# Routing by pairs of heads, a share of the expert rows on VectorE, and a respaced schedule in a two-layer diffusion step

## The chip, the cores and the metric

The kernel runs on one core of a Trainium2 chip. The metric is the device time of one execution in microseconds (us). Three runs of the kernel before took 2585.73, 2594.09 and 2606.0 us; the median, 2594.09 us, is the time that the change is held against.

## What is computed

The reference is one step of a two-layer network on 128 context tokens and 256 latent tokens, all in float32 with a model width of 1024. Each layer modulates its input, mixes the tokens (three parallel groups of heads: neighbourhood attention, grouped-query attention, a Fourier mix), projects, adds and normalizes; then it does the same with a mixture of small experts (PEER) in place of the token mix:

```python
x <- LN(ALPHA*x + gate1 * TokenMix(x*(1+scale1)+shift1))
x <- LN(ALPHA*x + gate2 * PEER(x*(1+scale2)+shift2))

q = (xt @ w_q).reshape(n, PEER_HEADS, 2, PEER_QHALF)          # 8 heads, 2 halves
s = jnp.einsum('nhpc,hpkc->nhpk', q, sub_keys)                # 128 keys per half
top_s, top_i = lax.top_k(s, 16)
cand_s = top_s[:, :, 0, :, None] + top_s[:, :, 1, None, :]    # 256 pairs per head
cand_i = top_i[:, :, 0, :, None] * 128 + top_i[:, :, 1, None, :]
best_s, best_j = lax.top_k(cand_s.reshape(n, 8, -1), 16)
experts = jnp.take_along_axis(cand_i.reshape(n, 8, -1), best_j, axis=-1)
gates = jax.nn.softmax(best_s, axis=-1)
a = einsum('tkd,td->tk', u_tab[experts], x)                   # 128 experts per token
y = einsum('tk,tkd->td', gates * gelu(a), v_tab[experts])
```

Each token so picks 128 of 16384 experts, and each expert is one row U (dotted with the token) and one row V (summed with the resulting weight). The six shift, scale and gate vectors of a layer come from a product of a conditioning vector with a 1024 x 6144 matrix ("modulation").

## The kernel before

**Blocks and stages.** The tokens stand in six blocks of 128: blocks 0 (context), 1 and 2 (latent) in layer 0, and blocks 3, 4 and 5, the same tokens in layer 1. A token mix runs once per layer for the context block and once for the two latent blocks together, so there are four mixes; the latent ones work on two blocks at once. A block's expert part has 128 "slots": slot k gathers, for each of its 128 tokens (one per partition), the k-th expert's U and V row, 8 KB, into one of the eight places of a ring (`uv_rows`, RING = 8, lines 358 and 585 to 592). The gathers are indirect transfers that GpSimd issues in order, and each waits until the place that it fills is free (line 588).

**What happens to a slot.** VectorE dots the U half with the token (`expert_dots`, line 1206); ScalarE makes the GELU, the weight and a diagonal matrix of the weights (`expert_weights`, lines 885 to 894); TensorE multiplies that diagonal with the V half and sums in PSUM in `acc` (`experts_sum`, lines 698 to 704), which also frees the slot. Two slots are one turn; TensorE is two turns behind (BEHIND). A block has 64 turns, numbered 0 to 63, and two more in which only TensorE works. The block's last step is `ln2` (line 1068): it waits for the sum and normalizes.

**The order of the work.** One list, SCHEDULE, is written out when the kernel is built (lines 152 to 204), and every engine goes through this same list in order, doing its own part of each step and waiting on semaphores. So each engine's instructions follow the order of the list, and a wait holds up all that stands behind it on that engine. The steps are `mod` (a tile of the modulation), `xT` (transpose and modulate), `proj` (an input projection tile), `norm`, `qkT`, `att`, `four`, `oT`, `gate`, `outp` (an output tile), `ln1`, `h2`, `wq` (a query tile of one head, and the key scores of the head before it), `top` (the 16 best of four lists of scores), `pick` (the routing's later part), `ln2` and `gather` (some turns of a block). `beside(q, steps, behind)` lays the turns of block q between the given steps: a fixed cost per kind of step (COST) says how far the turns must have come at each step, and `behind` turns are left over at the end. `filled_in` puts `mod` steps behind given kinds of steps (FILL). Beside block 0 stands the mix of blocks 1 and 2 and their queries; beside block 1 the routing of block 2, what is left of the modulation and the start of the mix of block 3; beside block 2 the rest of that mix and the queries; beside block 3 the mix of blocks 4 and 5; beside block 4 the routing of block 5; beside block 5 nothing.

**Routing.** For each pair of heads, `top` searches four lists and `pick` 0 to 3 adds the scores of 2 x 16 x 16 pairs and searches the best 16 per head (lines 1147 to 1154). Only then, for all eight heads at once, `pick` 4 and 5 turn the found positions into expert numbers by comparing with 0 to 15, multiplying and summing (lines 1159 to 1170), and make the gates. One signal, `route_ready`, then releases all 128 slots of the block to GpSimd (lines 581 and 1180).

**Weights.** SyncE issues the weight tiles of 1 MB in the order of the list into three places (`wtiles`). Up to the first gather the eight places of the ring serve as further weight places: the first EARLY_TILES tiles may use them, and GpSimd waits until these tiles are used (lines 311 and 583).

Of the kernel before, what the change touches and what calls it, by code (L numbers as in the profile page):

```python
# [31 lines left out]
U32 = mybir.dt.uint32  # L32
# [5 lines left out]
P = 128  # L38
# [12 lines left out]
PER_TOKEN = R_H * TOPK  # L51
ALPHA = (2 * DEPTH) ** 0.25
# [71 lines left out]
def query_steps(m):  # L124
# [7 lines left out]
    return steps + [("pick", q, 4), ("pick", q, 5)]  # L132


def route_steps(q):

    return [s for n in range(4) for s in (("top", q, n), ("pick", q, n))] + [("pick", q, 4), ("pick", q, 5)]
# [9 lines left out]
def cost(step):  # L147
    by_mix = step[0] in ("proj", "att", "outp", "wq", "four")
    return COST[step[0]][by_mix and len(BLOCKS[step[1]]) - 1] + 3 * (step[0] == "pick" and step[2] >= 4)

# [123 lines left out]
ROUTE = numbered(("pick",), lambda s: [s[1]] if s[2] == 5 else [])  # L274
# [10 lines left out]
def routes_before(step):  # L285

    return sum(s[0] == "pick" and s[2] == 5 for s in SCHEDULE[:SCHEDULE.index(step)])
# [23 lines left out]
EARLY_TILES = sum(s in TILES for s in SCHEDULE[:SCHEDULE.index(("xT", BLOCKS[1][0]))])  # L311
# [35 lines left out]
def hybrid_step(nc, i, o):  # L347

    ctx = ExitStack()
    with ctx:  # L350
# [42 lines left out]
        half_j = sb("half_j", [P, PER_TOKEN], U32)  # L393
        half_f = sb("half_f", [P, PER_TOKEN])
        picked = sb("picked", [P, 2, PER_TOKEN])
# [617 lines left out]
        def _(dve):  # L1013
# [127 lines left out]
            def pick_experts(q, part):  # L1141
# [29 lines left out]
                if part < 5:  # L1171
                    return
# [183 lines left out]
```

## Time and profile before

| | us |
|---|---|
| median of three runs | 2594.09 |
| profiled execution | 2596.99 |
| span of its one core | 2595.2 |
| TensorE busy (share of the span) | 2175.1 (84%) |
| VectorE busy | 1471.3 (57%) |
| ScalarE busy | 839.9 (32%) |
| GpSimd busy | 855.1 (33%) |
| bytes moved | 962.04 MB, mean 371 GB/s |

The profile is of one execution, and its page gives busy times per engine and the span in 40 slices of 64.9 us. Other views show single instructions in order of time, sums over stretches of time, groups of like instructions, and who waited for whom. PE is TensorE's matmuls, DVE is VectorE, ACT is ScalarE, POOL is GpSimd, SP is SyncE. A wait is shown in brackets behind the instruction that it delayed. PEclk is the granted TensorE clock as a share of 2.4 GHz.

### The profile page before, as it was taken

The numbers are of one execution on the slowest core, as the hardware profiler recorded it, in microseconds if no ns is written. First come the engines' busy times: TensorE is split into PE (matmuls) and PEld (weight loads), VectorE is DVE, ScalarE is ACT, GpSimd is POOL, SyncE is SP. The second block draws the span as 40 slices with busy tenths as digits, with TensorE's granted clock in tenths as the row PEclk, the third lists the DMA queues.
The fourth block names the chain that finished last, engine by engine and source line by source line (L and its number), as shares of the span: only waits on it lengthen the run. The fifth ranks groups of instructions, "written<-read, shape, count | busy, mean of one in ns | idle before, by whom it ended". The sixth has DMA issues, their size and how long they took to land.

```text
span 2595.2 us, 22854 instructions
## 1 busy us (share of the span) xinstructions
PE 2175.1 (84%) x7370; PEld 1179.5 (45%) x7370; DVE 1471.3 (57%) x3171; ACT 839.9 (32%) x2632; POOL 855.1 (33%) x772
## 2 busy tenths in 40 slices
PE   7997999899687888798887799999968786777775
PEld 5585655566232344354443465567523332323222
DVE  0146456456788544545668446644786767544444
ACT  2423366232222232443222237622222222222222
POOL 0001235222244443233444124422324444343331
PEclk8797999999798999899998899999979898999998
DMA  9958989799799999999999699979979999999996
GB/s 397 369 202 357 334 341 412 294 388 373 285 387 421 395 421 421 374 373 418 419 420 392 255 348 369 415 283 362 361 272 416 422 420 395 378 423 421 421 422 252
DMA packets 142631, 962.04 MB, mean 371 GB/s; under 512 B 15920, under 2 KB 24240, under 8 KB 28208
## 3 DMA queue, kind: packets, MB, share of 16 engines
q0 software_dynamic: 110592, 805.36, 76.7%
q1 hardware_dynamic: 30912, 152.06, 15.3%
q10 hardware_dynamic: 1008, 3.17, 0.3%
q8 instruction: 58, 0.95, 0.1%
q14 instruction: 61, 0.50, 0.0%
HBM read 958.17 MB, written 2.36 MB: 370 GB/s over the span
## 4 chain that ended last, share of the span: by engine, by line
PE 49%; DMA 26%; DVE 15%; issue 5%; ACT 3%; POOL 0%; SPq 0%; DVEq 0%; POOLq 0%; ACTq 0%
PE acc L701 27%; DMA uv_rows<-in_peer_uv,experts 25%; PE pair L757 8%; PE pair L816 6%; DVE products L1206 3%; PE pair L721 2%; PE pair L794 1%; PE pair L642 1%; DVE arena L1132 1%; PE pair L620 1%; DMA uv_rows<-in_w_mod 1%; ACT weight L889 1%; PE pair L731 1%; DVE arena L1167 1%; DVE arena L1169 1%
## 5 line engine op out<-in xcount | busy, mean ns | idle before, releaser
L701 PE MATMUL acc<-uv_rows,diag 128*128 128x512 f32 x3072 | 1474.6, 632 | 274.5 <-ACT diag L893 274.3
L589 POOL DMA_INDIRECT uv_rows<-in_peer_uv,experts x768 | 854.9, 1113 | 1702.2 <-PE acc L701 1372.2
L1206 DVE CUSTOM_DVE_ANT_0 products<-uv_rows,h_tok 128x1024 bf16<-128x1024 f32 x768 | 940.9, 1225 | 741.4 <-DMA uv_rows<-in_peer_uv,experts 730.5
L701 PEld LDWEIGHTS acc<-uv_rows,diag 128*128 128x128 f32 x3072 | 602.1, 202 | 1088.0 <-issue 677.0
L885 ACT ACTIVATE gelu<-dots 128x2 f32<-128x2 f32 x384 | 78.3, 204 | 1220.7 <-DVE dots L1206 1220.3
L893 ACT ACTIVATE diag<-consts,weight 128x128 f32<-128x128 f32 x768 | 260.2, 386 | 0.0
L757 PE MATMUL pair<-wtiles,hT 128*128 128x256 f32 x976 | 220.7, 385 | 13.3 <-ACT hT L849 13.3
L757 PEld LDWEIGHTS pair<-wtiles,hT 128*128 128x128 f32 x976 | 188.7, 194 | 52.9 <-issue 28.0
L889 ACT ACTIVATE weight<-gelu,gates 128x1 f32<-128x1 f32 x768 | 184.3, 287 | 12.6
L835 ACT COPY arena<-pair 128x256 f32<-128x256 f32 (+3 forms) x154 | 83.4, 549 | 281.0 <-PE pair L757 109.6
L816 PE MATMUL pair<-hT,wtiles 128*128 128x256 f32 (+1 forms) x864 | 154.2, 337 | 0.0
L816 PEld LDWEIGHTS pair<-hT,wtiles 128*128 128x128 f32 x864 | 137.9, 191 | 22.9 <-issue 10.5
L794 PE MATMUL pair<-arena,consts 128*128 128x512 f32 x40 | 34.1, 1004 | 51.5 <-DVE arena L1190 51.5
L885 ACT ACT_TABLE_LOAD x51 | 65.4, 1283 | 0.9
L1206 DVE DVE_READ_ACCUMULATOR2_ANT dots<- 128x1 f32 x768 | 63.1, 82 | 0.0
L721 PE MATMUL pair<-uv_rows,cond_s 128*32 128x256 f32 x576 | 53.8, 513 | 4.5 <-DMA uv_rows<-in_w_mod 2.1
L1031 DVE TENSOR_REDUCE maxes<-pair 128x2 f32<-128x768 f32 (+1 forms) x36 | 28.1, 780 | 50.6 <-PE pair L620 50.2
L864 ACT ACT_TABLE_LOAD x31 | 39.8, 1283 | 36.1 <-DVE neg_max L1032 36.0
L731 PEld LDWEIGHTS pair<-consts,mod_row 128*128 128x128 f32 x192 | 34.1, 256 | 35.8 <-issue 15.2
L1126 DVE MAX8 top_s<-arena 128x8 f32<-128x128 f32 x96 | 20.9, 280 | 49.1 <-ACT arena L835 49.0
L731 PE MATMUL pair<-consts,mod_row 128*128 128x2 f32 x192 | 37.1, 303 | 13.0 <-ACT mod_row L835 12.9
L1088 DVE TENSOR_REDUCE root_in<-arena 128x10 f32<-128x640 f32 x6 | 4.9, 820 | 72.7 <-ACT arena L946 72.7
(113 smaller groups left out, 1192.5 us busy)
## 6 DMA issues: line engine op xcount, KB each, us to landing
uv_rows<-in_w_mod SPq DMA_DIRECT2D x36, 1024.0 KB, 14.2
wtiles<-in_peer_wq SPq DMA_DIRECT2D x27, 1024.0 KB, 5.7
wtiles<-in_w_in SPq DMA_DIRECT2D x24, 1024.0 KB, 9.6
wtiles<-in_w_out SPq DMA_DIRECT2D x15, 1024.0 KB, 6.9
wtiles<-in_w_mod SPq DMA_DIRECT2D x12, 1024.0 KB, 12.3
uv_rows<-in_peer_uv,experts POOLq DMA_INDIRECT x768, 11.0
rows<-in_ln_g SPq DMA_DIRECT2D x12, 512.0 KB, 7.9
rows<-in_ln_b SPq DMA_DIRECT2D x12, 512.0 KB, 11.1
```

Source lines behind the costliest of these rows:

```text
L589: pool.indirect_dma_start(out=uv_rows[:, slot, :, :].rearrange("p t d -> p (t d)"), out_offset=None, in_=i["peer_uv"], in_offset=bass.Indi ...
L701: last = nc.tensor.matmul(acc[:, half, :], diag[:, slot, :], uv_rows[:, slot, 1, half * 512:(half + 1) * 512], start=False, stop=True, ski ...
L721: last = nc.tensor.matmul(dst[at:at + QUADRANT, 0, 0:TW], cond_s[:, k, :], w[:, k, :], start=(k < GROUPS_OF_PE), stop=(k >= NC - GROUPS_OF ...
L731: last = nc.tensor.matmul(dst[:, 0, 2 * k:2 * k + 2], mod_row[:, (t - 1) % 2, k * P:(k + 1) * P], const("halves"), start=True, stop=True)
L757: last = nc.tensor.matmul(dst, hT[:, k, b * P:(b + 1) * P], w[:, k, :], start=(k == 0), stop=(k == NC - 1))
L794: last = nc.tensor.matmul(dst[:, n, :], ones, z[:, n * 512:(n + 1) * 512], start=True, stop=True)
L816: last = nc.tensor.matmul(dst[:, h, 0:t], w[:, k, h * P:(h + 1) * P], hT[:, k, 0:t], start=(k == 0), stop=(k == NC - 1))
L835: last = nc.scalar.copy(out, src)
L885: nc.scalar.activation(gelu[:, slot:slot + G], dots[:, slot:slot + G], ACT.Gelu).then_inc(gelu_ready, 1)
L889: nc.scalar.activation(weight[:, slot + j:slot + j + 1], gelu[:, slot + j:slot + j + 1], ACT.Copy, scale=gates[:, q % 3, at:at + 1]).then_ ...
L893: nc.scalar.activation(diag[:, slot + j, :], ident, ACT.Copy, scale=weight[:, slot + j:slot + j + 1]).then_inc(diag_ready, 1)
L1206: nc.vector.tensor_tensor_reduce(out=products[:, :], in0=uv_rows[:, slot, 0, :], in1=h_tok[:, slot_q, :], scale=1.0, scalar=0.0, op0=ALU.m ...
```

## The change

Four things change.

1. A pair of heads is routed to its end in one `pick` step: position, expert numbers and gates of its 32 slots, from an area of 1024 elements instead of 2048 done twice. Each of the four steps signals `route_ready`, and GpSimd waits for it at every 32nd slot. The steps `pick` 4 and 5 are gone.
2. In blocks 0 and 3, of every four slots the last (n % 4 == 3) has its V row summed by VectorE in SBUF (`dve_sum`), one turn later, in place of the diagonal on ScalarE and the four matmuls on TensorE. `ln2` of these blocks adds the two sums.
3. The gathers of block 0 begin behind its first `pick`, with the other query and routing steps of that block laid between its turns. The weight places in the ring are given up before the first `wq` (EARLY_TILES is 43 instead of 64), so that the `wq` tiles have three places.
4. COST is changed, `behind` is 6, 1, 6, 6 and 6 instead of 2, 0, 3, 2 and 3, and no `mod` steps stand behind `top` and `pick` any more. Of the 48 modulation tiles 13 leave the start and 3 leave block 1; these 16 stand in block 2 now, between `oT` and `gate`, turns 10 to 25.

Unrolled, the list has so many turns of the block ahead of these steps (before / after). Block 0: first projection 0 / 10, attention from 9 to 33 / 19 to 33, output tiles 36 to 39 / 35 to 38, queries of blocks 1 and 2 from 44 / 43, last `pick` 62 / 58. Block 3: attention 12 to 35 / 14 to 30, output tiles 37 to 40 / 32 to 35, queries from 45 / 41, last `pick` 62 / 58. Beside block 0 after, each `top` and its `pick` for blocks 1 and 2 stand together, with two turns, a `wq`, a turn, a `wq` and a turn up to the next `top`; beside blocks 2 and 3 after, one turn or none stands between a `top` and its `pick`; beside blocks 1 and 4, three and five.

```diff
+PARTS = 4
+PER_PART = PER_TOKEN // PARTS
+PART_H = R_H // PARTS
...
-COST = {"mod": (3, 3), "bias": (2, 2), "xT": (3, 3), "proj": (4, 6), "norm": (4, 6), "qkT": (2, 2), "att": (3, 12),
-        "four": (0, 0), "kvout": (0, 0), "oT": (1, 1), "gate": (3, 3), "gate2": (0, 0), "outp": (4, 7),
-        "ln1": (3, 3), "h2": (4, 4), "wq": (4, 8), "top": (4, 4), "pick": (5, 5), "ln2": (4, 4)}
+COST = {"mod": (3, 3), "bias": (2, 2), "xT": (3, 3), "proj": (4, 7), "norm": (6, 6), "qkT": (3, 3), "att": (3, 8),
+        "four": (1, 2), "kvout": (0, 0), "oT": (2, 2), "gate": (3, 3), "gate2": (0, 0), "outp": (4, 7),
+        "ln1": (4, 4), "h2": (3, 3), "wq": (5, 8), "top": (5, 5), "pick": (9, 9), "ln2": (4, 4)}
...
-FILL = {"kvout": 1, "qkT": 1, "att": 2, "four": 1, "ln1": 3, "h2": 1, "top": 2, "pick": 5}
+FILL = {"kvout": 1, "qkT": 1, "att": 2, "four": 1, "ln1": 3, "h2": 1}
...
-    last = queries.index(("wq", 0, R_H))
-    s += filled_in(mix_end(0), fill, FILL) + queries[:last + 1] + filled_in(queries[last + 1:], fill, FILL)
-    s += beside(0, mix_start(1) + mix_middle(1) + mix_end(1) + query_steps(1), 2)
-
-    s += beside(1, route_steps(2) + fill + mix_start(2))
-    s += beside(2, mix_middle(2) + mix_end(2) + query_steps(2), 3)
-    s += beside(3, mix_start(3) + mix_middle(3) + mix_end(3) + query_steps(3), 2)
-    s += beside(4, route_steps(5), 3)
+    first = queries.index(("pick", 0, 0)) + 1
+    s += filled_in(mix_end(0), fill, FILL) + queries[:first]
+    s += beside(0, queries[first:] + mix_start(1) + mix_middle(1) + mix_end(1) + query_steps(1), 6)
+
+    before_mix, after = [t for t in fill if t[2] < PART_G1 or t[1] == 0], [t for t in fill if t[1] and t[2] >= PART_G1]
+    s += beside(1, route_steps(2) + before_mix + mix_start(2), 1)
+    s += beside(2, mix_middle(2) + after + mix_end(2) + query_steps(2), 6)
+    s += beside(3, mix_start(3) + mix_middle(3) + mix_end(3) + query_steps(3), 6)
+    s += beside(4, route_steps(5), 6)
...
+SHARED_WITH_DVE = (0, 3)
+def summed_by_dve(n):
+    return n // PER_TOKEN in SHARED_WITH_DVE and n % 4 == 3
...
-EARLY_TILES = sum(s in TILES for s in SCHEDULE[:SCHEDULE.index(("xT", BLOCKS[1][0]))])
+EARLY_TILES = sum(s in TILES for s in SCHEDULE[:SCHEDULE.index(("wq", 0, 0))])
...
-                pool.wait_ge(route_ready, ROUTE[q])
...
+                    if k % PER_PART == 0:
+                        pool.wait_ge(route_ready, PICK[(q, k // PER_PART)])
                     if n >= RING:
-                        pool.wait_ge(row_used, n - RING + 1)
+                        by_pe, by_dve = summed_before(n - RING + 1)
+                        if summed_by_dve(n - RING):
+                            pool.wait_ge(row_added, by_dve)
+                        else:
+                            pool.wait_ge(row_used, by_pe)
...
-                elif kind == "pick" and a[1] == 4:
-                    act.wait_ge(best_ready, ROUTE[a[0]])
+                elif kind == "pick":
+                    act.wait_ge(best_ready, PICK[a])
                     nc.scalar.activation(gate_e[:, :, :], gate_e[:, :, :], ACT.Exp).then_inc(gate_exp, 1)
...
+                        if q in SHARED_WITH_DVE:
+                            dve.wait_ge(row_added, summed_before(PER_TOKEN * (q + 1))[1])
+                            nc.vector.tensor_tensor(zz, acc[:, :, :], dve_sum[:, :].rearrange("p (a n) -> p a n", a=2),
+                                                    ALU.add).then_inc(acc_drained, 1)
+                            dve.wait_ge(acc_drained, q + 1)
+                            link(nc.vector.tensor_tensor(zz, zz, gate_b, ALU.mult))
...
+                top_sixteen([(flat[:, h], best_s[:, PART_H * part + h], best_j[:, PART_H * part + h]) for h in range(PART_H)])
+                nc.vector.tensor_tensor(gate_e[:, :, :], best_s[:, heads, :], spread(best_s[:, heads, 0:1], [P, PART_H, TOPK]),
+                                        ALU.subtract).then_inc(best_ready, 1)
+                nc.vector.tensor_copy(top_f[:, :, :], top_i[:, lists, :])
+                nc.vector.tensor_scalar(half_j[:, :, 0, :], best_j[:, heads, :], 4, None, ALU.logical_shift_right)
+                link(nc.vector.tensor_scalar(half_j[:, :, 1, :], best_j[:, heads, :], 15, None, ALU.bitwise_and))
+                link(nc.vector.tensor_copy(half_f[:, :], half_j[:, :, :, :].rearrange("p h f k -> p (h f k)")))
+                by_slot = hit.rearrange("p (n a) -> p n a", a=TOPK)
+                link(nc.vector.tensor_tensor(by_slot, spread(half_f[:, :].unsqueeze(2), [P, 2 * PER_PART, TOPK]),
+                                             spread(iota.unsqueeze(1), [P, 2 * PER_PART, TOPK]), ALU.is_equal))
...
+                dve.wait_ge(gate_exp, PICK[(q, part)])
...
+                def add_rows(h):
+                    for n in range(q * PER_TOKEN + h * G, q * PER_TOKEN + (h + 1) * G):
+                        if not summed_by_dve(n):
+                            continue
+                        slot, before = n % RING, summed_before(n)[1]
+                        dve.wait_ge(weight_ready, n + 1)
+                        if before:
+                            dve.wait_ge(row_added, before)
...
+                            nc.vector.scalar_tensor_tensor(out=dve_sum[:, :], in0=uv_rows[:, slot, 1, :],
+                                                           scalar=weight[:, slot:slot + 1], in1=dve_sum[:, :],
+                                                           op0=ALU.mult, op1=ALU.add).then_inc(row_added, 1)
...
+                    if 1 <= h <= GROUPS:
+                        add_rows(h - 1)
```

## Rows read from the trace of the kernel before

**Rows 1.** Page, GB/s per slice of 64.9 us, and all transfers

```profile
GB/s 397 369 202 357 334 341 412 294 388 373 285 387 421 395 421 421 374 373 418 419 420 392 255 348 369 415 283 362 361 272 416 422 420 395 378 423 421 421 422 252
...
DMA packets 142631, 962.04 MB, mean 371 GB/s; under 512 B 15920, under 2 KB 24240, under 8 KB 28208
```

**Rows 2.** Stretches, blocks 0 to 4: length, busy per engine, clock, DMA, GB/s

```profile
234.00:709.00 475.00, 434.71 (x1573) 270.95 (x1571) 267.56 (x575) 188.72 (x502) 152.97 (x136) 0.95 0.89 348
...
709.00:1061.00 352.00, 284.81 (x704) 129.48 (x704) 225.58 (x489) 97.74 (x357) 146.08 (x129) 0.92 1.00 409
...
1061.00:1446.00 385.00, 321.07 (x987) 165.25 (x987) 235.98 (x515) 125.41 (x406) 148.79 (x128) 0.91 0.98 395
...
1446.00:1921.00 475.00, 433.22 (x1579) 270.39 (x1578) 272.47 (x580) 187.34 (x498) 143.65 (x128) 0.95 0.86 331
...
1921.00:2255.00 334.00, 257.20 (x520) 104.61 (x520) 222.06 (x480) 87.67 (x327) 145.02 (x128) 0.91 0.99 407
```

**Rows 3.** Waits of GpSimd: us in total, times, longest

```profile
POOL uv_rows L589 <- DVE gates L1179: 52.0, 2, 26.4
```

**Rows 4.** Timeline, GpSimd, first gather: start, us, engine, line

```profile
233.64 1.07 POOL L589 DMA_INDIRECT uv_rows<-in_peer_uv,experts  x1 [233.19 <-PE pair L721]
```

**Rows 5.** Timeline, VectorE: routing of block 0, first dot product

```profile
177.85 0.69 DVE L1151 TENSOR_TENSOR arena<-top_s 128x512 f32<-128x512 f32 x1
...
182.92 0.88 DVE L1126 MAX8 top_s<-arena 128x8 f32<-128x128 f32 x4
...
188.26 0.69 DVE L1151 TENSOR_TENSOR arena<-top_s 128x512 f32<-128x512 f32 x1
...
230.83 0.29 DVE L1179 TENSOR_TENSOR gates<-gate_e,gate_n 128x128 f32<-128x128 f32 x1
...
239.76 1.22 DVE L1206 CUSTOM_DVE_ANT_0 products<-uv_rows,h_tok 128x1024 bf16<-128x1024 f32 x1 [8.65 <-DMA uv_rows<-in_peer_uv,experts]
```

**Rows 6.** Timeline, TensorE: a turn, a query tile, two attention steps

```profile
488.12 3.60 PE L701 MATMUL acc<-uv_rows,diag 128*128 128x512 f32 x8
...
562.27 7.07 PE L816 MATMUL pair<-hT,wtiles 128*128 128x256 f32 x32
...
569.17 1.05 PE L825 MATMUL pair<-sktiles,arena 128*128 128x128 f32 x8
...
1094.13 0.49 PE L620 MATMUL pair<-kT,qT 64*128 64x128 f32 x4 [2.07 <-ACT arena L835]
...
1100.50 0.49 PE L620 MATMUL pair<-kT,qT 64*128 64x128 f32 x4
```

**Rows 7.** Groups by line and form: busy us, mean ns of one

```profile
L1071 DVE SCALAR_TENSOR_TENSOR arena<-x_tok,arena 128x1024 f32<-128x1024 f32 x12 | 14.7, 1225 | 0.4
...
L849 ACT ACTIVATE hT<-pair,mod_cols 128x128 f32<-128x128 f32 x96 | 34.5, 472 | 15.8 <-PE pair L610 15.8
```

**Rows 8.** Stretches of block 0, and the attention of block 3

```profile
240.00:315.00 75.00, 73.65 (x277) 53.92 (x278) 35.17 (x63) 22.26 (x57) 17.52 (x15) 0.96 0.97 362
...
315.00:458.00 143.00, 139.64 (x537) 77.17 (x538) 82.42 (x152) 90.76 (x223) 66.10 (x53) 0.99 0.93 371
...
537.00:648.00 111.00, 111.00 (x437) 77.52 (x436) 67.78 (x208) 28.26 (x92) 28.91 (x29) 1.00 0.97 377
...
648.00:709.00 61.00, 38.74 (x68) 15.46 (x66) 42.66 (x94) 14.45 (x41) 16.17 (x17) 0.78 0.70 279
...
1541.00:1682.00 141.00, 139.37 (x551) 77.39 (x549) 82.44 (x152) 93.76 (x230) 64.24 (x54) 1.00 0.97 382
```

**Rows 9.** Timeline, VectorE, block 4: last routing step to next dot

```profile
2185.35 0.22 DVE L1165 TENSOR_SCALAR half_j<-best_j 128x128 uint32<-128x128 uint32 x1
...
2194.31 1.22 DVE L1206 CUSTOM_DVE_ANT_0 products<-uv_rows,h_tok 128x1024 bf16<-128x1024 f32 x1
```

**Rows 10.** Stretch behind that step

```profile
2200.00:2210.00 10.00, 10.00 (x23) 4.35 (x23) 5.54 (x10) 3.22 (x13) 4.69 (x5) 0.94 0.84 302
```

**Rows 11.** Timeline, TensorE behind a wait, end of block 3

```profile
1885.83 6.01 PE L701 MATMUL acc<-uv_rows,diag 128*128 128x512 f32 x8 [8.96 <-ACT diag L893]
```

More of the change, by code:

```diff
@@ L148, in cost @@
     by_mix = step[0] in ("proj", "att", "outp", "wq", "four")
-    return COST[step[0]][by_mix and len(BLOCKS[step[1]]) - 1] + 3 * (step[0] == "pick" and step[2] >= 4)
+    return COST[step[0]][by_mix and len(BLOCKS[step[1]]) - 1]
 def beside(q, steps, behind=0):
@@ L285, in routes_before, with summed_before @@
 def routes_before(step):
-    return sum(s[0] == "pick" and s[2] == 5 for s in SCHEDULE[:SCHEDULE.index(step)])
+    return sum(s[0] == "pick" for s in SCHEDULE[:SCHEDULE.index(step)])
+SHARED_WITH_DVE = (0, 3)
+def summed_by_dve(n):
+    return n // PER_TOKEN in SHARED_WITH_DVE and n % 4 == 3
+def summed_before(n):
+    by_dve = sum(summed_by_dve(k) for k in range(n))
+    return n - by_dve, by_dve
 def mix_of(q):
@@ L1142, in pick_experts @@
                 l, slot = q // 3, q % 3
-                c4 = cand.rearrange("p (h a b) -> p h a b", h=R_H, a=TOPK)
-                top4 = top_s[:, :, :].rearrange("p (h f) k -> p h f k", f=2)
-                shape = [P, R_H, TOPK, TOPK]
-                top_f = scores[:, place_in_mix(q), 0:2 * R_H * TOPK].rearrange("p (h f k) -> p h f k", f=2, k=TOPK)
-                if part < 4:
-                    heads = slice(2 * part, 2 * part + 2)
-                    two = [P, 2, TOPK, TOPK]
-                    link(nc.vector.tensor_tensor(c4[:, heads], spread(top4[:, heads, 0, :].unsqueeze(3), two),
-                                                 spread(top4[:, heads, 1, :].unsqueeze(2), two), ALU.add))
-                    flat = cand.rearrange("p (h n) -> p h n", h=R_H)
-                    top_sixteen([(flat[:, h], best_s[:, h], best_j[:, h]) for h in (2 * part, 2 * part + 1)])
@@ L1171, in pick_experts @@
-                if part < 5:
-                    return
-                link(nc.vector.scalar_tensor_tensor(out=picked[:, 0, :], in0=picked[:, 0, :], scalar=float(KEYS),
-                                                    in1=picked[:, 1, :], op0=ALU.mult, op1=ALU.add))
-                link(nc.vector.tensor_scalar(experts[:, slot, :], picked[:, 0, :], float(l * EXPERTS), None, ALU.add))
-                dve.wait_ge(gate_exp, ROUTE[q])
+                heads = slice(PART_H * part, PART_H * (part + 1))
@@ new lines, in pick_experts @@
+                lists = slice(2 * PART_H * part, 2 * PART_H * (part + 1))
+                c4 = cand.rearrange("p (h a b) -> p h a b", h=PART_H, a=TOPK)
+                top4 = top_s[:, lists, :].rearrange("p (h f) k -> p h f k", f=2)
+                shape = [P, PART_H, TOPK, TOPK]
+                link(nc.vector.tensor_tensor(c4, spread(top4[:, :, 0, :].unsqueeze(3), shape),
+                                             spread(top4[:, :, 1, :].unsqueeze(2), shape), ALU.add))
+                flat = cand.rearrange("p (h n) -> p h n", h=PART_H)
@@ L1181, in pick_experts @@
-                dve.wait_ge(route_ready, ROUTE[q])
+                nc.vector.tensor_tensor(gates[:, slot, at].rearrange(by_head, h=PART_H), gate_e[:, :, :],
+                                        spread(gate_n[:, :].unsqueeze(2), [P, PART_H, TOPK]), ALU.mult).then_inc(route_ready, 1)
+                dve.wait_ge(route_ready, PICK[(q, part)])
             def gate_on_diagonals(key):
```

70 lines of the change are left out of this document (38 added, 32 removed).

## Prediction

> **What bounds the kernel now.** I began with the page's slices. The 962 MB that the core moves would take 2285 us at the 421 GB/s of the full slices [rows 1], so about 310 us of the 2595 us span are time in which the transfers are not full, and the question is which stretches lose them. The busy times by block answer it [rows 2]. Blocks 1, 2 and 4 run at 409, 395 and 407 GB/s: they are bound by the transfers, and TensorE has room. Blocks 0 and 3, beside which the two-block mixes run, are the slow ones, 475 us each at 348 and 331 GB/s, with TensorE busy for 435 and 433 us: they are bound by TensorE. The waits add one thing: GpSimd waited twice, 52 us together, for the end of the routing of the next block (blocks 1 and 4) [rows 3]. The start is bound by the routing of block 0: the first gather goes out at 233.6 us [rows 4], just behind the end of that routing at 230.8 us, while the modulation tiles run beside it [rows 5].
>
> **Prices.** One gathered row, one weight tile and one modulation tile are 1.049 MB each by their shapes, so 2.49 us of transfer at 421 GB/s; a turn (two rows) is 4.98 us. On TensorE a turn is 3.44 us (3.60 with the pipeline's tail), a tile of a two-block mix 6.9 us (32 matmuls, as a query tile's), a query tile 7.8 us with its key scores [rows 6]. With every fourth row on VectorE, a turn costs TensorE 2.58 us on average.
> On VectorE the top-16 search of two heads is 5.3 us and one combination step 5.1 us [rows 5]. The new step ends the routing of its pair as well: three operations on 1024 elements at 1.23 us [rows 7] and some ten small ones at about 0.2 us (an estimate from the 0.29 us of a 128-element one [rows 5]), so 10.9 us. Per block that is 4 x 16.2 = 65 us against 58 before: little in sum, but in one piece of 10.9 us. The V addition is 1.23 us too, by the nearest operation of its form [rows 7]; half and double that are its bounds, since its scalar comes from memory and no row has that.
>
> **Start and block 0.** The first combination begins at 177.9 us [rows 5]; plus 10.9 us, the first gather goes out at 189 us, 45 us sooner. What follows is VectorE's: three more pairs (3 x 16.2), 18 dot products at 1.27 us, four additions (5 us), behind 6.1 us until the first row lands [rows 4, 5]. That ends at about 275 us. ScalarE has its part of turn 8 ahead of the 16 modulations at up to 0.47 us [rows 7], so the first projection tile starts at about 284 us instead of 240. Then, against the stretches of before [rows 8]:
> projection, 7 x 6.9 + 8 x 2.58 = 69 us (75 before);
> attention, 143 us with 26 turns leaves 50 us of TensorE's own work, so 50 + 16 x 2.58 = 91 us. Where one turn stands beside a step the chain score, maximum, exponential, transpose may set the pace: in block 2 such a step repeats after 6.4 us [rows 6], which makes 14 x 6.4 and the Fourier and transposing work, about 104 us. I take 97;
> output and first norm, 79 us before (458 to 537), 78 after: four turns fewer rows for TensorE, but two norms closer together on VectorE;
> queries and rest, 111 + 61 = 172 us before. Now a pair's search and combination stand together with nothing between. After a combination TensorE waits for the first turn's dots (2.5), ScalarE's weights (1.3), does that turn (3.4) and a query tile (7.8), and only then can VectorE search again (16.2): 31.6 us for two tiles and four turns, where TensorE alone needs 25.9 and VectorE alone 28.8. With 28 us to the first search, 16 us, three rounds (the last 4 us shorter) and 24 us of last rows it makes 159 us.
> Block 0 so ends at 284 + 69 + 97 + 78 + 159 = 687 us instead of 709: **-22 us**. The 45 us of the early start and TensorE's savings mostly go into VectorE's order.
>
> **The moved modulation tiles.** Thirteen tiles leave the start, where they were hidden under the routing and cost nothing, and with three of block 1 they stand in block 2. Block 2's transfers are at 395 of 421 GB/s [rows 2], so their cover is gone: 16 x 2.49 = **+40 us** there, **-7.5 us** in block 1. Its idle transfers, about 20 us by these rates, lie in attention, ahead of the place of the tiles; filled, they would make it 20, which is the lower bound. SyncE issues the tiles into the same three buffers one after another; the output and query tiles queue behind them, which the transfers' own time covers.
>
> **Longer steps in the blocks bound by transfers.** In block 4 VectorE left the rows alone for 9.0 us once [rows 9], and the slice behind it fell to 302 GB/s, a loss of 2.8 us [rows 10]; steps of 5.3 us there cost nothing (417 to 421 GB/s [rows 1]). The ring of 8 rows covers the rest. On this line 10.9 us lose 4.2 us; 2 and 10 us are the bounds (10 if search and combination act as one, 16 us less what the ring holds). Twelve such steps in blocks 1, 2 and 4: 51 us, less 14 that the old ends of these blocks lost (4.7 us each: on the same line, one step of 9.0 us and one some 1.5 us shorter): **+37 us**.
>
> **Block 3.** Stretches as in block 0: attention 141 us with 24 turns, now 18: 103 us [rows 8]; projection and output about 5 us less, norms 10 more, for turns moved there; queries and rest stay at 165 us, since with a turn between search and combination the query tiles run ahead. With the wait at its end gone inside that: **-31 us**. Both ends with a routing wait leave the next block with an empty ring; filled, blocks 1 and 4 gain some **-5 us** together beyond it.
>
> **Edits at nothing or little.** The extra addition of the two sums ahead of the second norm of blocks 0 and 3, 2 x 1.23 = **+2.5 us**, stands on the path. GpSimd's four waits for a release per block instead of one find it given a block ahead, except in block 0; if not, the old 26 us return. ScalarE's exponentials, four per block instead of one, run beside VectorE's selection; without that cover each would hold VectorE 2 to 3 us. A VectorE row is free only behind the next turn's dots, some 4 us later than by TensorE; the ring covers it where transfers have slack.
>
> **Sum:** -22 + 40 - 7.5 + 37 - 31 - 5 + 2.5 = +14 us. The profiled execution took 2596.99 us, 2.9 above the median of 2594.09: 2611 on its scale, **2608 us** on the median's.
>
> **Rivals.**
> Faster: TensorE, not VectorE's order, sets blocks 0 and 3. For it: 111 us of 111 busy in the query stretch of before [rows 8]. Then that stretch and its rest take 8 x 7.8 + 16 x 2.58 + 27 = 131 us instead of 159 and 165: -62 us, 2546 us; if the ring also hides the long steps, some 2520. Against it: the search needs the key scores, and they stand behind the rows that the combination holds up.
> Slower: VectorE's additions lie on the path everywhere. It decides from the point where VectorE, going in order, comes to a turn after its rows have landed. The forecast has about half of the 64 additions beside other work; put on the path they are 32 x 1.23 = 39 us, 2647 us. For it: VectorE gets the longer steps and the additions in the same stretches. Against it: it was busy 268 of 475 us [rows 2].
> Slower too: TensorE, idling between rounds, loses its clock. After a wait of 9 us eight matmuls took 6.0 us [rows 11] instead of 3.6 [rows 6], and the last stretch of block 0, which has such waits, was granted 0.78 of the clock [rows 8]: between 2.4 us and a whole query tile at 1.2 GHz (6.9) in each of seven rounds, +17 to +65 us, 2625 to 2673 us.
> The Trainium skill, "TensorE: Matmul & The Clock Gate", section "HAM oscillation — how this bites in real kernels", warns that an array left idle between bursts begins each burst at the slow clock: it speaks against work taken from TensorE, and by that rule the seven rounds would stand at the upper of these times; the row agrees for the first turn only.
> Not as said: the first release does not come early, because the five query tiles ahead of it now share three buffers and wait for one another; with the first gather some 16 us later, 2624 us.
>
> **Chances.** The forecast 42 in 100, by itself 2583 to 2635 (bounds of the long steps, of attention and of the tiles); the faster rival 28, the additions 18, the clock 9, no early release 3. What a measurement can tell from no change is 1%, 26 us: faster is below 2568, slower above 2620. Faster: 2 of the forecast's 42, 24 of the faster rival's 28: 0.26. Slower: 10, 18, 6 and 2 of the others: 0.36. The rest, 0.38, is within. The range 2540 to 2660 leaves out the far ends of the faster rival and of the clock.
>
> **What would show it.** Right: first gather near 189 us; first projection tile near 284; no wait of GpSimd for the gates; query stretches of blocks 0 and 3 with VectorE busy and TensorE waiting for the diagonals; block 2 some 55 us longer than 385, at over 400 GB/s; slices near 300 behind the combinations of block 4. Wrong: block 0 ending before 660 us, or the query stretches with TensorE still full, or block 2 hardly longer.

## The result and the profile after

The changed kernel takes 2655.8 us (median of 4 runs, 2645.5 to 2661.5); the kernel before, run beside it, 2591.2. The ratio is 1.0236, interval 1.0182 to 1.029: slower, though the interval leaves open whether by more than 2%. The profiled execution took 2654.3 us with a span of 2652.5, 57.3 more than before. 2608 had been forecast, with a range of 2540 to 2660.

The page of the changed kernel, GB/s per slice of 66.3 us and all transfers, answers to [rows 1]:

```profile
GB/s 397 381 212 323 309 340 307 334 309 342 341 364 394 397 421 422 351 411 392 366 406 405 270 366 361 330 337 346 339 358 381 390 385 389 402 405 422 422 421 262
DMA packets 142633, 962.05 MB, mean 363 GB/s; under 512 B 15920, under 2 KB 24240, under 8 KB 28208
```

The bytes are the same; the slices of block 4 (the 31st to 35th) stand at 381 to 402, where before most stood at 416 to 422. By block (from one addition of the expert rows to the next; block 0 from the first gather; columns as in [rows 2]):

```profile
178.65:697.55 518.90, 403.29 (x1558) 265.19 (x1558) 354.57 (x828) 195.44 (x494) 159.62 (x134) 0.89 0.85 326
697.55:1056.93 359.38, 280.22 (x644) 128.60 (x644) 231.65 (x524) 104.37 (x357) 139.62 (x129) 0.90 0.97 395
1056.93:1497.09 440.16, 353.43 (x1307) 183.88 (x1307) 241.76 (x550) 143.90 (x463) 141.15 (x128) 0.88 0.95 384
1497.09:1963.24 466.15, 388.42 (x1450) 250.96 (x1450) 314.00 (x647) 185.16 (x475) 148.75 (x127) 0.91 0.87 335
1963.24:2312.99 349.75, 251.34 (x520) 101.55 (x520) 228.19 (x516) 95.98 (x336) 143.00 (x129) 0.91 0.95 391
```

Block 0 ends 11.2 us earlier than before (708.8), block 1 takes 7.5 us more, block 2 54.5 more, block 3 8.6 less, block 4 15.7 more, and the last block the same. So the loss is in block 2 and in the other blocks that transfers bound; the gain in blocks 0 and 3 is small. The release works as said. GpSimd's timeline of the changed kernel, first gather, answering to [rows 4]:

```profile
178.65 1.08 POOL L616 DMA_INDIRECT uv_rows<-in_peer_uv,experts  x1 [178.20 <-DVE gates L1212]
```

Its waits (us in total, times, longest), answering to [rows 3]: that for the gates is the first one alone, and a new one, for the slots that VectorE sums, has come.

```profile
POOL uv_rows L616 <- DVE gates L1212: 178.2, 1, 178.2
POOL uv_rows L616 <- DVE dve_sum L1244: 78.9, 11, 13.1
```

**Block 2.** The stretch with the moved modulation tiles: transfers full, TensorE and VectorE with time to spare.

```profile
1116.95:1222.17 105.22, 82.42 (x401) 37.45 (x401) 32.49 (x54) 25.76 (x110) 28.31 (x26) 0.82 1.00 414
```

**A long step in block 4.** VectorE's timeline of the changed kernel, last dot before an ending, its first and last operation, next dot (answering to [rows 9]):

```profile
2075.63 1.23 DVE L1255 CUSTOM_DVE_ANT_0 products<-uv_rows,h_tok 128x1024 bf16<-128x1024 f32 x1 [1.25 <-DMA uv_rows<-in_peer_uv,experts]
...
2076.78 0.69 DVE L1186 TENSOR_TENSOR arena<-top_s 128x512 f32<-128x512 f32 x1
...
2087.23 0.19 DVE L1212 TENSOR_TENSOR gates<-gate_e,gate_n 128x32 f32<-128x32 f32 x1
2087.46 1.23 DVE L1255 CUSTOM_DVE_ANT_0 products<-uv_rows,h_tok 128x1024 bf16<-128x1024 f32 x1
```

The stretches around it, columns as in [rows 2], answering to [rows 10]:

```profile
2080.00:2085.00 5.00, 1.66 (x4) 0.38 (x2) 4.79 (x14) 1.51 (x2) 1.88 (x2) 0.94 1.01 419
2085.00:2090.00 5.00, 0.00 (x0) 0.00 (x0) 4.69 (x12) 0.01 (x1) 0.00 (x0) 0.50 1.01 421
2090.00:2095.00 5.00, 3.95 (x5) 1.72 (x6) 4.90 (x8) 2.53 (x10) 0.00 (x0) 0.54 0.60 247
2095.00:2100.00 5.00, 5.00 (x13) 2.28 (x12) 2.54 (x6) 2.53 (x10) 3.50 (x3) 1.00 0.66 242
2100.00:2110.00 10.00, 10.00 (x24) 4.18 (x22) 4.43 (x7) 1.26 (x5) 7.18 (x6) 1.00 0.99 380
```

The step holds VectorE for 10.7 us (10.9 forecast). All eight slots of the ring are full behind it, so the next dots wait for nothing, GpSimd issues nothing from 2085 to 2095 (x0), and the transfers run dry: at 421 GB/s the three last stretches lose 2.1 + 2.1 + 1.0 = 5.2 us.

**The query rounds of block 3** in the changed kernel, the same stretch as 537 to 648 of block 0 in [rows 8]:

```profile
1789.92:1904.62 114.70, 101.16 (x402) 72.02 (x400) 87.84 (x248) 31.26 (x87) 31.71 (x32) 0.97 0.90 352
```

TensorE's expert rows in it, behind a wait, with the query tile that follows, and without one (answering to [rows 11]):

```profile
1869.91 3.39 PE L730 MATMUL acc<-uv_rows,diag 128*128 128x512 f32 x4 [8.12 <-ACT diag L924]
1873.13 7.07 PE L845 MATMUL pair<-hT,wtiles 128*128 128x256 f32 x32
...
1897.32 1.88 PE L730 MATMUL acc<-uv_rows,diag 128*128 128x512 f32 x4
```

Before, such a stretch took 111 us and TensorE was busy in all of it. Now it waits 13.5 us, about as much as its rows had become cheaper, and VectorE is busy for 87.8.

### The profile page after: what moved, and what is told of

Its sections match the earlier page's. It is cut to its first block, busy times and chain, and to the rows that moved or that the text cites. A ratio compares the mean times of both kernels' runs of the same rounds, so it can differ in the third digit from the quotient of the medians.

```text
span 2652.5 us, 22706 instructions
## 1 busy us (share of the span) xinstructions
PE 2071.0 (78%) x7114; PEld 1133.8 (43%) x7114; DVE 1576.6 (59%) x3447; ACT 865.5 (33%) x2622; POOL 852.3 (32%) x772
## 4 chain that ended last, share of the span: by engine, by line
PE 37%; DMA 26%; DVE 22%; issue 8%; ACT 6%; POOL 1%; SPq 0%; DVEq 0%; ACTq 0%; POOLq 0%
DMA uv_rows<-in_peer_uv,experts 25%; PE acc L730 19%; PE pair L786 8%; DVE products L1255 4%; PE pair L845 3%; DVE arena L1170 2%; PE pair L823 1%; ACT weight L918 1%; PE pair L750 1%; DVE arena L1197 1%; DVE arena L1200 1%; DVE picked L1202 1%; PE pair L647 1%; ACT diag L924 1%; DVE top_i L1167 1%
## 5 line engine op out<-in xcount | busy, mean ns | idle before, releaser
L730 PE MATMUL acc<-uv_rows,diag 128*128 128x512 f32 x2816 | 1374.4, 639 | 340.2 <-ACT diag L924 340.2
L730 PEld LDWEIGHTS acc<-uv_rows,diag 128*128 128x128 f32 x2816 | 556.2, 205 | 1085.9 <-issue 609.1
L924 ACT ACTIVATE diag<-consts,weight 128x128 f32<-128x128 f32 x704 | 241.5, 386 | 0.0
L918 ACT ACTIVATE weight<-gelu,gates 128x1 f32<-128x1 f32 x768 | 184.2, 287 | 12.6
L845 PE MATMUL pair<-hT,wtiles 128*128 128x128 f32 (+1 forms) x1024 | 172.9, 327 | 1.4 <-DMA sktiles<-in_sub_keys 1.4
L845 PEld LDWEIGHTS pair<-hT,wtiles 128*128 128x128 f32 x1024 | 156.5, 191 | 26.7 <-issue 12.7
L1244 DVE SCALAR_TENSOR_TENSOR dve_sum<-uv_rows,weight,dve_sum 128x1024 f32<-128x1024 f32 x62 | 79.4, 1280 | 13.6 <-ACT weight L918 13.6
L1062 DVE TENSOR_REDUCE maxes<-pair 128x2 f32<-128x768 f32 (+1 forms) x36 | 28.1, 780 | 54.1 <-PE pair L647 53.9
L854 PE MATMUL pair<-sktiles,arena 128*128 128x128 f32 x192 | 29.4, 293 | 27.4 <-ACT arena L864 27.4
## 6 DMA issues: line engine op xcount, KB each, us to landing
uv_rows<-in_w_mod SPq DMA_DIRECT2D x26, 1024.0 KB, 13.5
rows<-in_ln_b SPq DMA_DIRECT2D x12, 512.0 KB, 11.2
```

The lines of the kernel that those rows point to most:

```text
L730: last = nc.tensor.matmul(acc[:, half, :], diag[:, slot, :], uv_rows[:, slot, 1, half * 512:(half + 1) * 512], start=False, stop=True, ski ...
L845: last = nc.tensor.matmul(dst[:, h, 0:t], w[:, k, h * P:(h + 1) * P], hT[:, k, 0:t], start=(k == 0), stop=(k == NC - 1))
L918: nc.scalar.activation(weight[:, slot + j:slot + j + 1], gelu[:, slot + j:slot + j + 1], ACT.Copy, scale=gates[:, q % 3, at:at + 1]).then_ ...
L924: nc.scalar.activation(diag[:, slot + j, :], ident, ACT.Copy, scale=weight[:, slot + j:slot + j + 1]).then_inc(diag_ready, 1)
L1244: nc.vector.scalar_tensor_tensor(out=dve_sum[:, :], in0=uv_rows[:, slot, 1, :], scalar=weight[:, slot:slot + 1], in1=dve_sum[:, :], op0=AL ...
```

## The experiments

All ratios are to the kernel before, run beside it on the same chip; its median lay between 2590.9 and 2594.5 us each time, so medians of different experiments are compared directly. Block lengths come from one profiled execution each; where two executions of the same block could be compared (block 3 of e4_two_picks and f1_two_picks_mods_early, one code, 462.4 and 456.4 us) they differ by up to 6 us.

**e1_no_sharing**

```
-SHARED_WITH_DVE = (0, 3)
+SHARED_WITH_DVE = ()
```

> The changed kernel with no row summed by VectorE; TensorE sums all 128 of every block again. Theory (sharing is worth its VectorE time, the loss is elsewhere): TensorE gets 32 rows of about 1.43 us back in each of blocks 0 and 3; outside the attention, which transfers set, that is on the path: 20 to 30 us per block, so about 2655 + 50 = 2705 us. Rival (the 62 additions of 1.28 us stand on the path): faster than 2655 by up to 79 us, about 2590 to 2640.

2671.1 us, ratio 1.032 [1.0274, 1.0366]: 15 us slower than the changed kernel, not 50 (the two intervals overlap a little, but the slowest run of the changed kernel, 2661.5, is below the fastest here, 2670.0). The additions are not the loss, so that rival falls; but they bring a third of what theory gave them. Block 3, which the additions shorten from 475.9 to 466.2 us:

```profile
1502.30:1978.20 475.90, 432.07 (x1578) 270.22 (x1578) 276.87 (x616) 194.65 (x507) 145.28 (x128) 0.95 0.86 330
```

**e2_sharing_alone**

```
 (kernel before: its schedule, costs and pick_experts)
+SHARED_WITH_DVE = (0, 3)
+    summed_by_dve, add_rows, dve_sum, and the waits on row_added
```

> The kernel before with the sharing alone (blocks 0 and 3), its schedule, its modulation tiles and its routing as they were. Theory: every turn of the TensorE-bound stretches of blocks 0 and 3 is shorter by about half a row, 0.86 us on some 40 of 64 turns, less what VectorE's order takes: 25 to 30 us per block, 2535 to 2565 us. Rival (additions on the path): 2591 to 2650 us.

2561.8 us, ratio 0.9885 [0.9849, 0.9922]: 32 us faster, within the theory's range, though not by its amounts per block. Block 3 is 19 us shorter (455.5) and block 0, from its first gather on, 11 us (464.0), where 25 to 30 had been expected of each; in the profiled execution another 14 us lie ahead of the first gather (last section). Its query rounds and the stretch behind them:

```profile
1719.37:1816.93 97.56, 97.56 (x398) 70.86 (x397) 69.65 (x206) 23.05 (x75) 27.63 (x27) 1.00 0.95 376
1816.93:1874.67 57.74, 27.82 (x53) 10.92 (x51) 48.52 (x99) 13.83 (x40) 15.18 (x15) 0.70 0.66 260
```

Here TensorE is busy throughout the rounds, and what it is spared shows: 97.6 us, against 109.6 in the same rounds before. VectorE has 18 us less to do in them than in the changed kernel.

**e3_mods_early**

```
-FILL = {..., "ln1": 3, "h2": 1}
+FILL = {..., "ln1": 4, "h2": 5}
-    s += beside(0, queries[first:] + mix_start(1) ...
+    rest = queries[first:last] + filled_in(queries[last:], fill, {"top": 5, "pick": 6})
+    s += beside(0, rest + mix_start(1) ...
```

> The changed kernel with the 16 modulation tiles of block 2 put back ahead of block 1's rows: 10 more steps between the first normalization and the first queries, 11 behind the last queries of block 0. Theory (they lost their cover in block 2, 440 us instead of 386): block 2 gets 40 to 54 us shorter; the first gather comes up to 17 us later (10 steps of 1.7 us on TensorE) and block 0 takes about 10 more, so 2625 to 2640 us. Rival (block 2 is long through its picks, and the tiles find no cover at the start either): 2650 to 2670 us.

2636.9 us, ratio 1.0139 [1.008, 1.0199]: 19 us better than the changed kernel, with runs from 2613.5 to 2648.1, of which the profiled one is the slowest. Block 2 falls from 440.2 to 399.6 us (-40.6); the first gather comes at 197.9 and block 0 ends at 728.8, 31 us later (16 of them are a later start than f1_two_picks_mods_early had with the same tiles there, last section):

```profile
1090.20:1489.80 399.60, 320.58 (x987) 165.39 (x987) 241.40 (x551) 134.08 (x415) 147.80 (x128) 0.89 0.95 382
```

So the tiles did cost 40 us in block 2, and at the start they are not free any more either.

**e4_two_picks**

```
-  steps += [("top", q, n), ("pick", q, n)]
+  steps += [("top", q, n), ("pick", q, n), ("last", q, n)]
-  "pick": (9, 9)
+  "pick": (5, 5), "last": (5, 5)
     (pick: the sums and top_sixteen; last: everything behind them)
```

> The changed kernel with each ending cut in two steps, the search (about 5 us) and the rest (about 6 us), so that expert turns can stand between them. Theory (a piece of 10 to 11 us on VectorE empties the ring where transfers set the time): 3 to 4 us less for each of the 12 endings of blocks 1, 2 and 4, and something in blocks 0 and 3, so 2605 to 2630 us. Rival (the ring is not emptied, or refills without loss): 2645 to 2660 us.

2589.4 us, ratio 0.9989 [0.9962, 1.0017]: 66 us faster than the changed kernel, more than theory gave. Its blocks 1 and 4:

```profile
681.70:1025.50 343.80, 278.55 (x644) 127.01 (x644) 231.34 (x525) 104.49 (x357) 142.35 (x129) 0.93 1.00 413
...
1917.20:2249.90 332.70, 263.98 (x520) 107.94 (x520) 227.78 (x516) 95.98 (x336) 141.68 (x129) 0.88 1.00 411
```

And its block 4 around the second search (2025.4 to 2030.6) and behind the rest of that ending (2045.7 to 2050.8):

```profile
2030.00:2035.00 5.00, 1.10 (x2) 0.50 (x2) 4.86 (x11) 2.78 (x7) 0.94 (x1) 0.75 1.02 424
...
2040.00:2045.00 5.00, 5.00 (x13) 2.13 (x13) 2.50 (x5) 1.27 (x5) 3.14 (x3) 1.00 1.01 421
...
2050.00:2055.00 5.00, 1.32 (x3) 0.50 (x2) 4.76 (x11) 1.27 (x5) 2.33 (x2) 0.79 1.01 421
```

The same VectorE work with turns between, and the transfers never leave 419 to 424 GB/s. Blocks 1, 2 and 4 give 15.6, 10.8 and 17.1 us: 43.5 for twelve endings, 3.6 each. Block 0 ends 15.8 us earlier, and block 3 gives 3.8 us: that is the part theory had left vague.

**f1_two_picks_mods_early** (the edits of e3_mods_early and e4_two_picks together)

> Endings in two steps (as in e4_two_picks) and the 16 modulation tiles ahead of block 1's rows (as in e3_mods_early). Theory (two separate losses): they add, 2589 - 19 = 2570 us; block 2 about 385 to 390 us, the first gather at 198, block 0 ending at 700 to 715. Rival (with short pieces the ring also covers the tiles in block 2): the tiles bring nothing more, 2585 to 2610 us.

2566.4 us, ratio 0.9909 [0.9879, 0.9939]; block 2 at 381.1, block 0 ending at 705.2. The total is the theory's, but the first gather came at 181.5 instead of 198, so part of it is the start (last section). The two losses add in the total and not block by block: in block 2 the tiles cost 48.3 us here (429.4 in e4_two_picks), and against e3_mods_early the short steps give 18.7, 18.5 and 16.8 us in blocks 1, 2 and 4, 4.5 for each of the twelve endings.

**f2_two_picks_no_sharing** (e4_two_picks with SHARED_WITH_DVE empty)

> Endings in two steps, no row summed by VectorE. Theory (the 10 us pieces, which e1_no_sharing still had, had eaten half of what sharing brings): slower than e4_two_picks by some 30 us, as much as e2_sharing_alone brought: 2615 to 2630 us. Rival (sharing is worth the 15 us of e1_no_sharing with the changed order, whatever the pieces): 2600 to 2608 us.

2608.1 us, ratio 1.0067 [1.0043, 1.0092]: sharing brings 19 us in the changed order by the medians, about as much as with long steps. It misses the theory's 2615 to 2630, by 7 us; the rival's value is met at its edge. Block 3 without sharing but with short steps:

```profile
1465.90:1929.20 463.30, 429.73 (x1578) 268.93 (x1578) 277.00 (x616) 195.62 (x507) 141.02 (x128) 0.97 0.88 339
```

That is 12.6 us less than e1_no_sharing, and no more than e4_two_picks with sharing (462.4): with short steps sharing shortens block 3 by 1 us and block 0, from the first gather on, by 13 (516.5 against 503.8).

**f3_old_order** (e4_two_picks with build_schedule, FILL and COST of the kernel before) and **f4_two_picks_old_costs** (e4_two_picks with COST and the margins of the kernel before)

> Sharing, and endings by pairs in two steps, in the order and with the costs of the kernel before: all queries of block 0 ahead of its rows, the modulation tiles there too, the first gather when they are used. Theory: block 2 at 382, block 1 at 344, blocks 0 and 3 as in e2_sharing_alone: 2545 to 2555 us. Rival (endings by pairs cost VectorE more in all than one ending for all heads): 2562 to 2575 us.

> As e4_two_picks (endings in two steps, early release, tiles in block 2), with the costs and the margins at the end of the kernel before; only the spreading differs. Theory (the costs move turns about and little time): 2580 to 2600 us. Rival (the spreading by trace times takes the gain of blocks 0 and 3): block 3 at 455 as in e2_sharing_alone, block 0 earlier by 5 to 10, 2565 to 2577 us.

2576.9 us, 0.9943 [0.9916, 0.9971], and 2596.8 us, 1.0018 [0.9994, 1.0041]. f3 misses its theory and lies 2 us above its rival's range: with the old order, endings by pairs are 15 us slower than one ending for all heads (e2). The rival's reason is not what the profile shows. The time is lost at the start: the first gather comes at 240.8 (219.3 in e2), and block 0 from there is the same, 464 us; why the start is longer was not tested. Three of the modulation tiles still stand in block 1 there, as in the kernel before, and it took 350.0 us where 344 had been expected. f4 meets its theory: the new costs are worth 7 us, with intervals that overlap. Block 3 takes 458.9 and 459.5 us.

**h1_last_later**

```
 (f1_two_picks_mods_early, blocks 1 and 4 only)
-  wq, wq, top, pick, last, wq, wq, top, pick, last, ...
+  wq, wq, top, pick, wq, wq, top, pick, ..., last, last, last, last
 (all blocks: the exponentials of the gates start in last instead of pick)
```

> As f1_two_picks_mods_early, with the second steps of the endings of blocks 1 and 4 (routed beside the query rounds of blocks 0 and 3) set behind the last query round instead of in it. Theory (in the rounds VectorE's endings keep TensorE waiting: 101.2 us busy of 114.7 in block 3 of the changed kernel, 97.6 of 97.6 in e2_sharing_alone): the rounds of block 3 shrink from 117 to 98 to 102 us, the stretch behind them grows by less, and blocks 0 and 3 each end 3 to 10 us earlier: 2550 to 2562 us. Rival (the time of rounds and rest together is set by the sum of the work, wherever the endings stand): the rest grows by as much, 2562 to 2572 us.

2585.9 us, ratio 0.9981 [0.9944, 1.0019]: 20 us slower than f1 and outside both ranges. The rounds of block 3 and what is behind them:

```profile
1732.09:1829.65 97.56, 97.56 (x399) 70.71 (x397) 72.25 (x209) 24.01 (x79) 28.61 (x28) 1.00 0.97 386
1829.65:1910.96 81.31, 47.91 (x85) 18.89 (x84) 67.70 (x156) 25.06 (x68) 25.53 (x24) 0.75 0.78 300
```

With the endings out of the rounds TensorE never waits, as the theory said, and they take 97.6 us instead of f1's 116.8. The gain is not: the stretch behind them grows from 54.9 to 81.3 us, and the block from 456.4 to 462.5. Sixteen of the 20 us are something else, the first gather (181.5 in f1, 197.8 here), although the steps of both kernels are alike up to there. The same stretch of the start in f1:

```profile
140.00:160.00 20.00, 19.08 (x217) 15.09 (x218) 0.00 (x0) 8.59 (x30) 0.00 (x0) 1.00 0.63 223
```

and in h1:

```profile
140.00:160.00 20.00, 19.51 (x134) 11.72 (x135) 0.00 (x0) 7.82 (x28) 0.00 (x0) 0.50 0.41 160
```

TensorE was granted full speed in one and half in the other, and did 217 matmuls against 134.

**h2_tiles_in_gaps**

```
 (f1_two_picks_mods_early)
-  wq 0, wq 1, wq 2, top, pick, last, wq 3, ...
+  wq 0, tile, wq 1, tile, wq 2, tile, top, pick, last, wq 3, tile, ...
```

> As f1_two_picks_mods_early, with the 16 modulation tiles set singly between the query tiles of block 0 (uses of tiles counted in their own order for that), some 3 ahead of them and the rest behind. Theory (beside VectorE's routing of block 0 TensorE stands idle about half of 89 us, so 1.7 us per step there costs nothing): block 0 ends 8 to 15 us earlier than the 705 of f1, 2551 to 2560 us. Rival (each stands in the chain from query to VectorE and delays it): 2562 to 2575 us.

2612.0 us, ratio 1.0074 [1.0046, 1.0102]: 46 us slower than f1 and outside both ranges. TensorE's waits from 120 to 345 us:

```profile
PE pair L776 <- DMA wtiles<-in_w_mod: 51.2, 8, 9.2
```

In f1 that wait is 6.6 us (120 to 305). Among the queries the tiles share three buffers with the query tiles, and each comes too late.

**h4_old_order_short**

```
 (e2_sharing_alone; one ending for all heads)
-  ("pick", q, 4), ("pick", q, 5)
+  ("pick", q, 4), ("pick", q, 5), ("pick", q, 6), ("pick", q, 7)
-FILL = {..., "h2": 1, "top": 2, "pick": 5}
+FILL = {..., "h2": 3, "top": 2, "pick": 3}
```

> As e2_sharing_alone (order and routing of the kernel before, rows shared), with the ending for all heads cut in four steps of 3 to 6 us instead of two of about 8, and the three modulation tiles that stood in block 1 put ahead of block 0's rows too. Theory (pieces over 5 us and tiles cost time where transfers set it): block 1 down from 354 to 343 to 346, blocks 2 and 4 by 2 each, the first gather up to 4 us later: 2545 to 2553 us. Rival (pieces of 8 us do not empty the ring, the tiles cost as much at the start): 2558 to 2566 us.

2558.9 us, ratio 0.9881 [0.9834, 0.9927], no different from e2. Block 1 did fall from 353.7 to 342.9 us and blocks 2 and 4 by 1.6 and 2.9, but block 0 ended at 697.9 instead of 683.3 (the first gather came at 230.7 instead of 219.3) and block 3 took 5.3 more; two edits share what block 1 gained, and this run does not part them.

**k1_shared_in_rounds**

```
 (h4_old_order_short, summed_by_dve, k = n % PER_TOKEN)
-  n % 4 == 3
+  every = 4 if k < 84 else 2 if k < 112 else 0
+  every > 0 and k % every == every - 1
```

> As h4_old_order_short, with VectorE's rows of blocks 0 and 3 placed by the stretch: every fourth of rows 0 to 83, every second of rows 84 to 111 (the query rounds, where TensorE was busy 95 of 99 us and VectorE 66), none of the last 16 (where VectorE was busy 50 of 58 us and TensorE 32). Theory (a shared row pays where TensorE is the busy engine and costs where VectorE is): the rounds of block 3 shrink from 99 to 87 to 93 us, the last stretch from 58 to about 53, so 2535 to 2548 us. Rival (TensorE and VectorE wait on one another in turn, wherever the rows go): 2553 to 2566 us.

2551.6 us, ratio 0.983 [0.9806, 0.9855]: the fastest of all, 7 us under h4, with intervals that overlap. Its rounds of block 3:

```profile
1730.18:1826.46 96.28, 84.49 (x365) 64.45 (x364) 72.98 (x206) 19.17 (x64) 31.12 (x28) 0.96 0.95 375
```

The rounds go from 99.2 to 96.3 us only, though TensorE's busy time in them falls by 10.6; the rest goes from 57.5 to 56.3. The time lies between the two ranges, 1 us below the rival's; the rival has the better of it.

## Why the prediction was right or wrong

The direction and the range held; the centre was 48 us too low. That the range held was luck: the bounds of the forecast's own terms were 2583 to 2635, which do not reach the time, and the rest of the range was room left for the rivals. By its own sum (profiled executions: +14 forecast, +57 measured):

**The tiles** (+40 in block 2): right. e3 takes 40.6 us off block 2 by moving them alone, f1 48.3 against e4. Their transfers fill it (414 GB/s while they run).

**Longer steps** (+37 net in blocks 1, 2 and 4): the mechanism is shown by e4, the net size was low. The three blocks together grew by 77.7 us, where tiles, steps and refilled ring had been put at 64.5. Taken off the 40.6 of the tiles, and with the 7.5 that block 1 was to save, steps cost about 45 net. The gross price was right: 51 us forecast, 43.5 given back in e4 and 53.9 in f1 against e3. The credits were too large. The 14 us that the old ends were to have lost and the 5 us of a refilled ring should have left f1, which has no long steps, 19 us below the kernel before in these three blocks, beside the 7.5 of the tiles; it is 7.8 us below.

**Block 0** (-22): -11. The first gather came at 178.7 (189 forecast) and the first projection at 267 (284), so the early start was better than forecast. It was lost behind: the norm stretch took 85 us (78), queries and rest 175 (159). (The forecast's round of 31.6 us is 31.2 by its own terms, 2.5, 1.3, 3.4, 7.8 and 16.2, and its end of VectorE's work at 275 us is 272: small beside this.) And the early start as such is worth little: block 0 ends at 681.7 in e4, which starts at 178 and has the tiles taken out, and at 683.3 in e2, which starts at 219 with most of them already done.

**Block 3** (-31): -8.6. This is the step that failed: that TensorE's spared rows shorten every stretch of this block. TensorE was busy 45 us less (433.2 to 388.4), but it waited 36 us more (41.8 to 77.7). The stretch from the first projection tile to the first output tile, and the one from the first query tile to the end of the block, columns as in [rows 2], before and then after:

```profile
1466.17:1689.26 223.09, 217.62 (x834) 133.91 (x835) 116.31 (x211) 114.43 (x284) 80.47 (x68) 0.98 0.92 355
1755.94:1921.03 165.09, 144.21 (x494) 90.78 (x492) 107.80 (x296) 41.28 (x127) 43.78 (x42) 0.92 0.83 323
...
1516.94:1713.57 196.63, 179.42 (x734) 116.14 (x735) 120.67 (x205) 103.50 (x244) 72.64 (x58) 0.96 0.92 352
1789.92:1963.24 173.32, 138.14 (x473) 88.19 (x471) 133.68 (x355) 48.27 (x138) 53.14 (x50) 0.89 0.87 340
```

Projection and attention became 26.5 us shorter, where the forecast took 38 off attention alone and 5 off projection and output. Output and norm grew by 9.7, about as forecast. Queries and rest, forecast at 165 because query tiles would run ahead of the ending, took 173. Attention did not follow TensorE's price per turn: in e2, where nothing else changes, TensorE is busy 16 us less between the last projection tile and the first output tile (126.7 against 142.8), and that stretch takes 146.9 us against 148.3, with a DMA share of 0.98 in both. In the rounds of the changed kernel TensorE waits: 101.2 us busy of 114.7, and in e1, with all rows its own, 113.5 of 116.8, so what it is spared there turns into waiting.

That the pairs' endings stand in the rounds is one reason (h1 takes the wait away), but the endings do not decide the block's length. f4 and e4 have the same steps and differ in costs and margins alone; the same two stretches in f4 and then in e4:

```profile
1485.50:1702.20 216.70, 197.94 (x767) 125.18 (x768) 135.52 (x227) 110.12 (x268) 80.49 (x67) 0.93 0.92 361
1773.17:1925.40 152.23, 124.16 (x449) 82.12 (x447) 120.38 (x337) 43.67 (x120) 45.41 (x41) 0.91 0.83 325
...
1474.70:1674.80 200.10, 182.71 (x735) 117.66 (x736) 119.54 (x204) 104.56 (x245) 69.08 (x56) 0.95 0.89 338
1742.89:1917.24 174.35, 146.36 (x482) 91.05 (x480) 139.66 (x364) 51.39 (x148) 55.39 (x52) 0.88 0.90 356
```

With the new costs 11 gathers leave the first stretch (67 to 56 on GpSimd) and 11 more stand in the second (41 to 52); the first is 17 us shorter, the second 22 longer, and the blocks take 459.5 and 462.4 us. So turns moved out of attention were paid for again among the queries. Taking the endings out of the rounds (h1) or spreading the rows otherwise (k1) also makes a stretch shorter and the block not. With sharing and short steps block 3 took 455 to 463 us in all eight kernels that had both, under three orders and two sets of costs. What sets that floor, with TensorE busy 384 to 396 and VectorE 310 to 314 us, stays open.

**The addition's price** (1.23 us, by an operation without a scalar from memory): nearly right, by the group of the changed kernel (busy, mean ns of one, idle before it).

```profile
L1244 DVE SCALAR_TENSOR_TENSOR dve_sum<-uv_rows,weight,dve_sum 128x1024 f32<-128x1024 f32 x62 | 79.4, 1280 | 13.6 <-ACT weight L918 13.6
```

**Rivals.** The additions rival's 2647 us is close to the time, and the clock rival's range holds it, but neither mechanism made the loss: without the additions the kernel is slower by 15 us (e1), and with them alone faster by 32 (e2). The faster rival fails, TensorE waits. The clock is a part, by an estimate: 32 rows off TensorE should leave 433 - 32 x 1.72 = 378 us in block 3, and it was busy for 388 with 0.91 of the clock granted instead of 0.95, so about 10 us, under the 17 to 65 of that rival. By the Trainium skill, "TensorE: Matmul & The Clock Gate", section "HAM oscillation — how this bites in real kernels", bursts after idling begin slow; the trace agrees with that for the first rows (four matmuls in 3.39 us instead of 1.88 behind a wait of 8.1), while the rounds as a whole were granted 0.97. The query tile behind that wait took its full-speed 7.07 us, so the upper price of that rival, a whole query tile at the slow clock in each round, was not paid there.

**What beat both.** Neither release nor order: sharing alone (e2) brings 32 us, and k1, with one ending for all heads in short steps, the tiles at the start and rows shared by stretch, 43 us.

## What to carry to other kernels

Hold the longest piece of work on the consuming engine against the depth of the ring before moving work into one step: here eight rows cover a step of 5 us entirely and one of 10.7 us at a loss of 3.6 to 5 us, and cutting the step in two gave 66 us without removing anything, 43.5 of them in the three blocks that transfers bound. Work beside idle transfers is cheaper than in a block bound by transfers: the same 16 tiles cost their full transfer time, 40 us or more, in block 2, and ended block 0 23 us later when they were put back ahead of it and into it (f1 against e4). An engine relieved of work shortens a stretch only as long as the engine that feeds it is not given more in the same stretch, and a shorter stretch need not make a shorter block: look at the block's end (f4 and e4, h1, k1).

## What was not expected of the hardware

TensorE's granted clock in the start differs between kernels that are alike up to there: from 140 to 160 us 1.00 in f1 and 0.50 in h1 and e3, whose first gathers come 16 us later. Not all of that is the clock: f1 was 4 us ahead by 45 us already, when its granted clock was no higher; the other 12 us came between 124 and 153 us. In the kernel before, it was 0.50 from 80 to 100 us though TensorE was busy throughout, and the first gather came at 233.6, against 219.3 in e2 with the same start. What makes the difference stays open, and so does whether every execution of a kernel has the same pattern; f1's and h1's medians differ as their profiled executions do. Block 0 is better read from the first gather on.
